# Forty of 128 first keys dense in place of 32, with seven places for rows of the second matrix and gates in groups of eight tokens

## The reference, cut to what matters

```python
s1 = jnp.einsum('thd,hkd->thk', q1, sub_keys_1)      # 8 heads, 128 first keys
s2 = jnp.einsum('thd,hkd->thk', q2, sub_keys_2)      # 128 second keys
v1, i1 = lax.top_k(s1, 16)
v2, i2 = lax.top_k(s2, 16)
cand = v1[..., :, None] + v2[..., None, :]           # 256 pairs
top_s, top_pos = lax.top_k(cand.reshape(t, 8, 256), 16)
expert_idx = ...                                     # i1 * 128 + i2 of the best 16 pairs
gates = jax.nn.softmax(top_s, axis=-1)
u = jnp.take(expert_u, idx, axis=0)                  # (token, head, 16, 2048)
hid = jax.nn.gelu(jnp.einsum('thkd,td->thk', u, xb)) * g
out = jnp.einsum('thk,thkd->td', hid, jnp.take(expert_v, idx, axis=0))
```

## Time and profile before

| | us |
|---|---|
| time, median of 3 executions | 3041.51 (3037.57 to 3043.05) |
| the profiled execution, its time | 3040.75 |
| its span, first to last instruction | 3038.8 |
| PE busy in the span | 2655.8 (87%) |
| DVE busy | 1834.4 (60%) |
| ACT busy | 1190.2 (39%) |
| POOL busy | 863.1 (28%) |

### The profile page before, as it was taken

One profiled execution on the slowest core, in us unless ns is written; L12 is line 12 of the kernel. 1 busy time (PEld: TensorE's weight loads), 2 busy tenths in 40 slices (PEclk: granted clock), 3 DMA queues, 4 the chain that ended last, 5 costly groups with the idle time before them and its releaser, 6 DMA issues.

```text
span 3038.8 us, 42842 instructions
## 1 busy us (share of the span) xinstructions
PE 2655.8 (87%) x16156; PEld 2096.7 (69%) x16156; DVE 1834.4 (60%) x2544; ACT 1190.2 (39%) x2346; POOL 863.1 (28%) x566
## 2 busy tenths in 40 slices
PE   8999899999999998999999999888865567767773
PEld 7886699999999988989999898665542322222220
DVE  6888555555455555455445468888677764455455
ACT  1003443333333345435334444565455532222233
POOL 0000000000000000040000003655568887666676
PEclk9999999999999998999999999999976778888887
DMA  6342445555555553444555657999999999999998
GB/s 241 139 146 107 176 153 189 184 183 190 181 192 181 192 180 129 153 146 146 181 182 189 239 206 276 393 418 394 414 364 390 394 382 400 421 412 415 420 419 343
DMA packets 128300, 794.54 MB, mean 261 GB/s; under 512 B 30514, under 2 KB 30514, under 8 KB 31730
## 3 DMA queue, kind: packets, MB, share of 16 engines
q0 software_dynamic: 75424, 415.85, 34.1%
q1 hardware_dynamic: 52736, 376.92, 33.8%
HBM read 921.37 MB, written 4.19 MB: 305 GB/s over the span
## 4 chain that ended last, share of the span: by engine, by line
PE 53%; DMA 16%; DVE 13%; issue 9%; POOL 6%; ACT 2%; DVEq 1%; POOLq 0%; ACTq 0%
PE bank L1801 15%; PE bank L1803 14%; PE bank L1802 14%; DMA s_u<-in_expert_u,s_u_index 9%; DMA s_v<-in_expert_v,s_v_index 6%; PE bank L1895 4%; DVE s_u L1678 4%; POOL s_v L588 3%; POOL s_u L570 3%; PE bank L2252 2%; DVE s_cacc L1215 2%; DVE s_yrow L1362 1%; DVE s_w_lo L1118 1%; ACT s_w_hi L615 1%; PE bank L1937 1%
## 5 line engine op out<-in xcount | busy, mean ns | idle before, releaser
L1118 DVE TENSOR_TENSOR s_w_lo<-s_raw,s_w_hi 128x2048 fp32r<-128x2048 f32 x258 | 592.4, 2296 | 652.8 <-ACT s_w_hi L615 652.4
L615 ACT ACTIVATE s_w_hi<-s_raw 128x2048 fp32r<-128x2048 f32 x256 | 489.8, 1913 | 653.7 <-PE bank L1803 653.7
L1801 PE MATMUL bank<-s_a_hi,s_w_hi 128*128 128x256 f32 x2560 | 721.5, 282 | 7.9 <-DVE s_w_lo L1118 3.6
L1802 PE MATMUL bank<-s_a_lo,s_w_hi 128*128 128x256 f32 x2560 | 722.2, 282 | 0.0
L1803 PE MATMUL bank<-s_a_hi,s_w_lo 128*128 128x256 f32 x2560 | 721.4, 282 | 0.0
L2252 PE MATMUL bank<-s_v,s_spread 128*32 128x512 f32 x2048 | 325.4, 793 | 310.2 <-DMA s_v<-in_expert_v,s_v_index 307.4
L1801 PEld LDWEIGHTS bank<-s_a_hi,s_w_hi 128*128 128x128 f32 x2560 | 485.3, 190 | 15.3 <-issue 8.1
L1803 PEld LDWEIGHTS bank<-s_a_hi,s_w_lo 128*128 128x128 f32 x2560 | 486.2, 190 | 0.0
L1802 PEld LDWEIGHTS bank<-s_a_lo,s_w_hi 128*128 128x128 f32 x2560 | 482.1, 188 | 0.5
L588 POOL DMA_INDIRECT s_v<-in_expert_v,s_v_index x256 | 427.2, 1669 | 186.9 <-PE bank L2252 87.1
L570 POOL DMA_INDIRECT s_u<-in_expert_u,s_u_index x256 | 387.8, 1515 | 255.2 <-issue 119.5
(11 more groups left out here) (316 smaller groups left out, 3070.0 us busy)
## 6 DMA issues: line engine op xcount, KB each, us to landing
s_raw<-in_stream SPq DMA_DIRECT2D x292, 1024.0 KB, 4.7
s_raw<-in_expert_v SPq DMA_DIRECT2D x32, 1024.0 KB, 8.8
s_raw<-in_dense_u SPq DMA_DIRECT2D x29, 1024.0 KB, 8.9
s_u<-in_expert_u,s_u_index POOLq DMA_INDIRECT x256, 14.6
s_v<-in_expert_v,s_v_index POOLq DMA_INDIRECT x256, 14.7
s_panel_early<-in_dense_u POOLq DMA_DIRECT2D x3, 1024.0 KB, 11.3
s_xres<-in_x SPq DMA_DIRECT2D x2, 1024.0 KB, 6.0
out<-s_out_row SPq DMA_DIRECT2D x8, 256.0 KB, 4.7
```

The costliest lines, as they stand in the source:

```text
L615: act.activation(w_hi[s % 2][:, :], raw[s][:, :], ACT.Copy).then_inc(hi_ready, 1)
L1118: dve.tensor_tensor(w_lo[s % 2][:, :], raw[s][:, :], w_hi[s % 2][:, :].bitcast(f32), ALU.subtract)\
L1801: pe.matmul(dst, left[0], right[0], start=start, stop=False)
L1802: pe.matmul(dst, left[0], right[1], start=False, stop=False)
```

## The change

`DENSE` goes from 32 to 40, so 88 first keys are left to the gathers and 40 u panels and 40 v panels are loaded and multiplied. `ha` grows by 8 KB per partition, into the memory of the eighth place for rows of v, so `NV` goes from 8 to 7. Several of DVE's small tiles (`cand`, `cand_rest`, `sc_rest`, `iota_i`, `pick`) now share one piece of memory. Eight tokens x 40 keys fill 320 of the 512 columns of a bank: the gates go in 32 groups of eight tokens over banks 4 to 7, in place of 16 groups of sixteen over banks 6 and 7. The schedules move: u panels 3, 3 and then two in each of the iterations 2 to 18; routes in two of three groups, the last in group 18 in place of 15; slots transposed at 19 on PE and 20 on ACT; fours eight each in groups 20 to 23 and four each in 24 to 31; v panels three in two iterations, from 34 to 60.

```diff
-DENSE = 32
+DENSE = 40
...
 def route_in(g):
-    th = EARLY + g - g // 5
-    return th if g % 5 < 4 and th < TT * PH else None
+    th = EARLY + g - g // 3
+    return th if g % 3 < 2 and th < TT * PH else None
...
-    return range(6 + 26 * (i - 2) // 15, 6 + 26 * (i - 1) // 15) if i < 17 else range(0)
+    return range(6 + 2 * (i - 2), 6 + 2 * (i - 1)) if i < 19 else range(0)
...
 def token_fours_in(g):
-    if 18 <= g < 20:
-        return range(8 * (g - 18), 8 * (g - 17))
-    return range(4 * (g - 16), 4 * (g - 15)) if 20 <= g < 32 else range(0)
+    if 20 <= g < 24:
+        return range(8 * (g - 20), 8 * (g - 19))
+    return range(4 * (g - 16), 4 * (g - 15)) if 24 <= g < 32 else range(0)
...
 def v_panels_in(i):
-    return range(5 * (i - 34) // 4, min(DENSE, 5 * (i - 33) // 4)) if i >= 34 and 5 * (i - 34) // 4 < DENSE else range(0)
+    return range(3 * (i - 34) // 2, min(DENSE, 3 * (i - 33) // 2)) if i >= 34 and 3 * (i - 34) // 2 < DENSE else range(0)
...
-    NU, NV, NW, NH, BATCH, LAG = 5, 8, 4, 4, 4, 4
+    NU, NV, NW, NH, BATCH, LAG = 5, 7, 4, 4, 4, 4
...
-                for first in {4: (2, 3), 5: (5, 6), 6: (7, 4)}.get(k, ()):
+                for first in {4: (2, 3), 5: (4, 5), 6: (6,)}.get(k, ()):
...
             def gated(group):
-                b = 6 + group % 2
+                b = 4 + group % 4
...
-                dve.wait_ge(one_key_used, 4 * (group + 1))
-                some = ha[:, :, 16 * group:16 * (group + 1)]
-                dve.tensor_tensor(some, some, bank[b][:, :].rearrange("p (t g) -> p g t", t=16), ALU.mult).then_inc(bank_empty[b], 1)
+                dve.wait_ge(one_key_used, 2 * (group + 1))
+                some = ha[:, :, 8 * group:8 * (group + 1)]
+                dve.tensor_tensor(some, some, bank[b][:, 0:8 * DENSE].rearrange("p (t g) -> p g t", t=8), ALU.mult).then_inc(bank_empty[b], 1)
...
-                        if f >= 8 and f % 4 == 0:
-                            gated(f // 4 - 2)
+                        if f >= 8 and f % 2 == 0:
+                            gated(f // 2 - 4)
...
             def token_four(f):
-                b = 6 + f // 4 % 2
-                if f % 4 == 0:
-                    into(b, DENSE // 4 + 1 + f // 8)
+                b = 4 + f // 2 % 4
+                if f % 2 == 0:
+                    into(b, DENSE // 4 + (b > 5) + f // 8)
```

More of the change, by code:

```diff
@@ L128, in dense_block @@
 def dense_block(d):
-    return d + DENSE // 2 if d < DENSE // 2 else d - DENSE // 4 if d < 3 * DENSE // 4 else d - 3 * DENSE // 4
+    return d + 16 if d < DENSE - 16 else d + 24 - DENSE if d < DENSE - 8 else d + 8 - DENSE
 def score_row(th):
@@ L328, in two_layers @@
     u_slot = [place(f"s_u{i}", [128, D], before_group if i == 0 else ring0 + (1 + i) * 8 * K) for i in range(NU)]
-    free = [S + 8 * K, ring0 - 8 * K, ring0 + 48 * K, ring0 + 56 * K, S + 56 * K, ring0 + 64 * K + (KT * L * 4),
+    free = [S + 8 * K, ring0 - 8 * K, ring0 + 48 * K, ring0 + 56 * K, ring0 + 64 * K + (KT * L * 4),
             ring0 + 72 * K + (KT * L * 4), ring0 - 16 * K]
@@ L337, in two_layers, with spot @@
     room = [[S + 66 * K, 229368], [before_cols, before_ident], [before_ones, before_group], [before_wf, ring0 - 16 * K]]
-    def small(name, n, dt=f32):
+    def spot(n):
         size = (4 * n + 63) // 64 * 64
@@ L343, in small @@
                 piece[0] += size
-                return place(name, [128, n], piece[0] - size, dt)
-        raise MemoryError(name)
+                return piece[0] - size
+        raise MemoryError(n)
+    def small(name, n, dt=f32):
+        return place(name, [128, n], spot(n), dt)
     slots_t = [small(f"s_slots_t{t}", 3 * SLOTS) for t in range(TT)]
@@ L351, in two_layers @@
     one_key_late = small("s_one_key_late", 8 * NKEYS)
[L352 to L355, removed]
+    pick_at = spot(2 * TOPK * TOPK)
     pick = place("s_pick", [128, 2 * TOPK * TOPK], pick_at)
-    iota_i = small("s_iota_i", NKEYS, mybir.dt.int32)
+    cand = place("s_cand", [128, TOPK * TOPK], pick_at)
+    cand_rest = place("s_cand_rest", [128, TOPK * TOPK], pick_at + 4 * TOPK * TOPK)
+    iota_i = place("s_iota_i", [128, NKEYS], pick_at, mybir.dt.int32)
     iota_f = small("s_iota_f", NKEYS)
-    sc_rest = small("s_sc_rest", NKEYS)
+    sc_rest = place("s_sc_rest", [128, NKEYS], pick_at + 4 * TOPK * TOPK)
     val = small("s_val", 2 * TOPK)
@@ L580, in gather_v @@
                 if k == 4:
-                    pool.wait_ge(panel_used, NPANELS + 1 + 2)
-                if k == 5:
                     pool.wait_ge(xnt_ready, 1)
-                if k == 7:
+                if k == 6:
                     pool.wait_ge(res_taken, 1)
@@ L1047, in dense_hidden @@
                 act.wait_ge(panel_used, NPANELS + 1 + d + 1)
-                if d == 3 * DENSE // 4:
+                if d == DENSE - 8:
                     act.wait_ge(expert_ready, PH)
@@ L1075, in _ @@
             for g in range(ROUTES * GROUPS):
-                if g == 18:
+                if g == 20:
                     for t in range(TT):
@@ L1775, in _ @@
                             one_keys_late(f // 4)
-                    if g == 32 and turn < 2:
-                        gated(14 + turn)
+                    if g == 32:
+                        gated(28 + turn)
                 if g == 61:
@@ L2238, in token_four @@
                     own_2 = slice(token % 32 * DENSE, (token % 32 + 1) * DENSE)
-                    ins = pe.matmul(bank[b][:, token % 16 * DENSE:(token % 16 + 1) * DENSE], four[:, e * NKEYS:(e + 1) * NKEYS],
+                    ins = pe.matmul(bank[b][:, token % 8 * DENSE:(token % 8 + 1) * DENSE], four[:, e * NKEYS:(e + 1) * NKEYS],
                                     one_key_2[:, own_2], start=True, stop=True)
@@ L2264, in _ @@
                     dense_u_panel(d)
-                if i == 17:
+                if i == 19:
                     for t in range(TT):
@@ L2269, in _ @@
                     for b in (4, 5):
-                        into(b, DENSE // 4)
+                        into(b, DENSE // 4 + 8)
                     for b in (6, 7):
```

## The result

The changed kernel takes 3078.6 us (median of 4 runs, 3072.8 to 3085.1) against 3042.3 us before: 1.012 times as long, with a 95% interval of 1.0093 to 1.0147. That is 36 us more, where 3038 us with a range of 3012 to 3074 was forecast. The profiled execution took 3085.1 us, its span is 3083.2 us.

What follows compares the result with a forecast made beforehand. DMA was taken to bound the panel stretches, POOL the panel-free one. Groups 3 to 60 went from 1050.2 us to 325.6 + 238 + 483.3 = 1046.9, so -3.3 us and 3038 us, range 3012 to 3074.

Steps and rivals of the forecast that it cites:

- What bounds the kernel: Expert stage before the change: DMA engines limit the stretches with panels, POOL the one without, at 16.18 us per group.
- the DMA account: DMA engine time summed over gathers and panels; 88 rows instead of 96 cut a gather from 1.917 to 1.757 us.
- Seven places for rows of v: Fourth row's gather waits for the previous adds; group at least 0.9 us + landing + adds; priced at no added time.
- I take the low end in all three: Landings assumed short enough that the seven-place loop adds nothing: groups of 19.15, 16.2 and 17.9 us, including 1% above floor.
- B: Groups 24 to 33, four token fours each, no panels: forecast 16.2 us per group, set by POOL.
- C: Groups 34 to 60, with v panels: forecast 17.9 us per group, 483.3 us for 27, set by DMA.
- Rival 2: The seventh place decides through longer landings in the expert stage: +29 us, 3070 us; chance 0.25.
- A: Groups 3 to 19, with u panels: forecast 19.15 us per group, 325.6 us for 17, set by DMA.
- X: Groups 20 to 23, eight token fours each: forecast 19 us per group, DVE's 18.0 plus one late-table wait over four groups.
- rival 3: PE limits the u-panel stretch, adds taking 5.95 instead of 3.64 us: +14.5 us, 3053 us; chance 0.10.
- the small edits: Sparser routes make nothing late, shared tiles cost nothing; smaller gates add 4.5 us on DVE, counted in the eight-four groups.
- Rival 1: Every expert-stage stretch at its floor, panel-free groups falling to 15.5 us: -23 us, 3018 us; chance 0.34.

Runs made afterwards that it cites:

- the kernel without the early place: Changed kernel with an eighth place from row 80, a ninth from row 136 and a second late-key-table buffer, none for rows 7 to 39: 3034.1 us.
- an early eighth place: Changed kernel with an eighth place for rows 7 to 39 and from row 80, ninth from 136: 3044.9 us; with second late-key-table buffer too: 3033.8 us.
- The second buffer: Changed kernel, seven places, with a second, alternating buffer for the late key table alone: 3066.7 us, ratio 1.0068 to the kernel before.
- the places given back: Changed kernel with an eighth place for rows 7 to 39 and from row 80, and a ninth from row 136: 3044.9 us, ratio 1.0009.

## Why the prediction was wrong, point by point

**What bounds the kernel** held in part. The run with fewer rows left the panel-free stretch at 15.97 us per group, so bytes don't count there, as the forecast had it. It shortened the two stretches with panels by 0.92 and 0.50 us per group where the DMA account gives 1.28, so DMA is a limit of both but not the only one.

**The step that failed** is the last of "Seven places for rows of v": "I take the low end in all three". The loop was described as it is, with its place, its 0.9 us and its three limits, and then priced at nothing, on the ground that B shows a landing of 10.0 us at a nearly full DMA, below C's limit of 12.2. What the runs show in its place is a loop that is closed in every round. In the changed kernel's groups 35 to 60 the fourth row is issued 0.95 us behind the adds, the next adds start 13.2 us after that, and they take 4.6: 18.8 us per group, against 17.9 forecast. Two things stand in these 13.2 us. Where two panels lie between the adds (13 groups), they start 13.0 us after the issue, when PE is through with its 14 us of panels (in one of them a little later). Where one panel lies between them (12 groups), they wait for the row and start after 9.1 to 16.6 us, 14.0 on the mean. A round lasts as long as the longer of the two, and a row that lands early gives nothing back, so one mean landing held against one limit is not the test: in the run with seven places alone the fourth rows of C landed after 11.1 us on the mean, below the limit, and a group took 18.8 all the same. (The forecast also called 10.0 us the best landing of the trace; it is the median of B, where single rows landed in 7.3.) In B the low end was wrong by the forecast's own figures for the kernel before, 16.85 us, and this came true in the run with seven places (16.9); in the changed kernel with its fewer rows B is 16.06, as forecast. What the places cost the changed kernel is 17 us in C (505.8 against 488.5) and 13 in the tail (76.4 against 63.2, the time behind group 60 of the kernel without the early place, which has nine places there). The tail I had left out altogether, as outside the change, though the same wait runs to its last group.

**Rival 2** was what happened in its mechanism, in C and the tail. That its 3070 us come within 9 of 3078.6 is partly luck: it was 6 short in C, 9 in A, 8 in X and the tail was missing, and it was 8 too high in B. (Its landing of 14 in A gives 19.7 us per group, not 19.6.)

**A** was too low by 0.98 us per group, 16.6 in all. The larger part is a mis-sized term, the price of a gather. From the view of DMA queues of the changed kernel, 1950 to 2200 us, with 100 gathers and 26 panels:

```profile
q0 software_dynamic: 14595, 74.18, 73.4%
q1 hardware_dynamic: 3744, 27.26, 26.3%
```

A gather costs 0.734 x 250 / 100 = 1.835 us in place of the 1.757 forecast, a panel 2.53, so a group 14.68 + 5.06 = 19.7 us where 19.06 was reckoned. With the 0.6% that the forecast took off, that is 19.6 against its 19.15: 8 of the 16.6 us. The bytes fetched per gather went from 0.791 to 0.742 MB, by 6.2% and not by 8.3, and the time went down by 4.3% only. The other 9 us are open. They can be the seventh place, whose loop is closed here too (all fourth rows of groups 4 to 19 follow the adds by 0.9 us, none did before): the two traces with an early eighth place have A 6 and 7 us shorter. They can be rival 3, adds at the lower clock. No run tells the two apart. In C a gather costs 0.767 x 440 / 187 = 1.805 us by the same view, 0.4 us per group more than forecast, but DMA is not full there.

**X** was 21.5 and not 19. The forecast counted the late table's wait once in four groups, 5.1 us. It comes in each, 15.9 us in all, because the first four fours run at the lower clock in 7.2 us behind ACT's tables, and close a loop of 21.6 us through DVE. The second buffer shows it (17.45 us). The wait was named, with its queue behind it; what was missing was to follow it round into the next group.

**B and the small edits** came out as forecast: 16.06 against 16.2, with 133.75 us of gathers and 80 x 0.30 between them in 160.6, so POOL nearly full. Gates of 320 elements, sparser routes and shared tiles show no cost in the windows; none of them was tested by itself. The first dot of group 3 came 9.7 us earlier. I put that down to the sparser routes, which leave group 2 without one, since DVE is busy 44.7 us in the stretch before it and was 53.1.

**Rival 1**, everything at its floor, fell: even with the places given back the time is 3044.9. Against its 18.95 in A stands the dearer gather.

## What to carry to other kernels

When places are released in batches, count them in batches: two full batches of four let a whole period pass between release and need, seven put a release, a transfer and the work on it into one period. That sum must be compared with the period, stage by stage and round by round, with the landing times of a loaded queue and with the work that the waiting engine has to do anyway. A wait that is named in the account must be followed once around to see if it comes again in each round. And before a work split is moved to save bytes, see where bytes are the limit and what the memory that it takes was doing: here ten of 64 groups could not use the saving at all, the saved bytes alone were worth 29 us, and one place alone cost 35.

## What was not expected of the hardware

The gathers' cost fell less than their bytes: 6.2% fewer bytes per gather, 4.3% less time of the DMA engines in A. The packets of skipped rows are too short to explain it. The 8 KB packets of the gathers themselves were busy longer on the mean, 319 ns each in A against 313 before, with a median of 309 in both; why is open. In the groups 24 to 33 of the kernel before with fewer rows, the share is 0.97 at 366 GB/s, where the same groups before have 0.99 at 389: a DMA share near one doesn't mean that the engines move at their full rate. The landing of a gather with seven places was 10.0 us with no panels about and 13.0 with them (medians over all rows); what exactly a panel adds to it was not measured by itself.
